# A chunked delta rule with and without the product w: k'S taken off the values in place, under new order tables

## The reference, cut to what matters

```python
decay = exp(where(tri, g[:, None] - g[None, :], -inf))       # g: running sum of the log decay
lower = where(strict, beta[:, None] * (k @ k.T) * decay, 0)
rhs   = concat([v * beta, k * (beta * exp(g))])
u, w  = split(triangular_solve(lower, rhs, unit_diagonal=True))
# from chunk to chunk, S is the 128 x 256 state of the head:
v_new = u - w @ S
o     = (q * exp(g)) @ S + (q @ k.T * decay) @ v_new
S     = S * exp(g_last) + (k * exp(g_last - g)).T @ v_new
```

## Time and profile before

| | |
|---|---|
| median of three runs | 1504.52 us |
| profiled execution | 1505.05 us, its span 1503.2 us |
| granted TensorE clock, mean | 0.996 |
| TensorE busy | 1482.1 us, 99% of the span |
| VectorE, ScalarE, POOL busy | 62%, 49%, 17% |
| DMA | 127.21 MB, mean 85 GB/s |

### The profile page before, as it was taken

How to read it: one execution, slowest core, us unless ns; L and a number is a source line. 1 busy time by engine, 2 the same in 40 slices (tenths; PEclk the granted TensorE clock), 3 DMA queues, 4 the chain that set the end, 5 groups by cost and what they waited for, 6 DMA issues and landing times.

```text
span 1503.2 us, 20571 instructions
## 1 busy us (share of the span) xinstructions
PE 1482.1 (99%) x7595; PEld 1186.4 (79%) x7595; DVE 924.7 (62%) x1740; ACT 736.4 (49%) x1292; POOL 261.9 (17%) x430
## 2 busy tenths in 40 slices
PE   9999999999999999999998999999999999999998
PEld 7878888888778878888877887666778888888887
DVE  5867777777655468788886346554475243433467
ACT  5454455544552356666665234665455341423343
POOL 1034323344302015354430000000000000000000
PEclk9999999999999999999999999999999999999999
DMA  5321211121114342222321332121233233232321
GB/s 210 99 71 60 68 57 56 57 62 51 57 57 146 112 111 95 76 93 79 92 78 57 99 100 63 59 68 42 87 95 99 85 112 98 85 101 96 98 84 70
DMA packets 40163, 127.21 MB, mean 85 GB/s; under 512 B 4576, under 2 KB 9104, under 8 KB 40064
## 3 DMA queue, kind: packets, MB, share of 16 engines
q1 hardware_dynamic: 38112, 121.65, 25.6%
q0 software_dynamic: 1040, 3.27, 0.6%
q10 hardware_dynamic: 912, 0.99, 0.2%
HBM read 122.69 MB, written 2.15 MB: 83 GB/s over the span
## 4 chain that ended last, share of the span: by engine, by line
PE 91%; DVE 4%; ACT 3%; issue 1%; DMA 0%; POOL 0%; SPq 0%; DVEq 0%; ACTq 0%; POOLq 0%
PE ps L891 89%; PE ps L1292 1%; DVE wl L2058 1%; PE ps L1036 1%; ACT sp L1954 1%; ACT sp L1952 0%; ACT sp L1956 0%; ACT wh L1439 0%; DVE up L2212 0%; DMA wraw<-in_wa 0%; DVE xr L2648 0%; ACT xr L1719 0%; DVE L L2600 0%; PE ps L1131 0%; ACT L1680 0%
## 5 line engine op out<-in xcount | busy, mean ns | idle before, releaser
L891 PE MATMUL ps<-xr,wh 128*128 128x512 f32 x2720 | 875.1, 402 | 3.4 <-DVE xr L2648 2.4
L891 PEld LDWEIGHTS ps<-xr,wh 128*128 128x128 f32 x2720 | 498.1, 189 | 119.9 <-issue 22.2
L891 PE MATMUL ps<-xr,wl 128*128 128x512 f32 x1376 | 538.6, 391 | 0.0
L2058 DVE TENSOR_TENSOR wl<-wraw,wh 128x1024 fp32r<-128x1024 f32 x214 | 268.2, 1260 | 131.6 <-ACT wh L1439 130.6
L891 PEld LDWEIGHTS ps<-xr,wl 128*128 128x128 f32 x1376 | 258.7, 188 | 55.6
L1439 ACT ACTIVATE wh<-wraw 128x1024 fp32r<-128x1024 f32 x214 | 222.1, 1049 | 74.4 <-PE ps L891 73.0
L891 PE MATMUL ps<-xm,wh 128*128 128x512 f32 x640 | 197.8, 390 | 0.0
L891 PEld LDWEIGHTS ps<-xm,wh 128*128 128x128 f32 x640 | 119.5, 188 | 26.2 <-DVE xm L2734 1.6
L891 PE MATMUL ps<-xm,wl 128*128 128x512 f32 x320 | 124.6, 389 | 0.0
L2096 DVE SCALAR_TENSOR_TENSOR qkv<-cin,gains,qkv 128x512 f32<-128x512 f32 x96 | 76.0, 792 | 10.0 <-ACT qkv L1469 9.3
L2919 POOL TENSOR_TENSOR L<-L 128x256 f32<-128x256 f32 x44 | 49.5, 1149 | 147.2 <-ACT L L1855 147.2
(11 more groups left out here) (292 smaller groups left out, 1763.9 us busy)
## 6 DMA issues: line engine op xcount, KB each, us to landing
wraw<-in_wa SPq DMA_DIRECT2D x48, 512.0 KB, 3.5
wraw<-in_wb SPq DMA_DIRECT2D x32, 512.0 KB, 4.2
wraw<-in_wu SPq DMA_DIRECT2D x32, 512.0 KB, 3.5
wraw<-in_wd SPq DMA_DIRECT2D x32, 512.0 KB, 3.6
wraw<-in_wao SPq DMA_DIRECT2D x16, 512.0 KB, 3.6
wraw<-in_wbo SPq DMA_DIRECT2D x16, 512.0 KB, 4.2
wraw<-in_wc SPq DMA_DIRECT2D x16, 512.0 KB, 3.5
bias<-rel_rows SPq DMA_DIRECT2D x16, 256.0 KB, 3.8
```

Source lines behind the costliest of these rows:

```text
L891: return e.matmul(out, w, x, start=start, stop=stop, skip_group_check=True)
L2058: e.tensor_tensor(m.wl[:, i % N_SPLIT, :], m.raw[:, i % N_RAW, :], m.wh[:, i % N_SPLIT, :].bitcast(F), ALU.subtract).then_inc(s.wlo, 1)
```

## The change

The product w, its scaling kg and its copy wT go. Normalised k is kept in a tile of its own (`kc`, two buffers; before it was written back over the head's k). At chunk n >= 1 a new product *k* multiplies it with the state (256 columns, the upper half of bank 4), and VectorE adds it, times the negative decay `egn`, to the values in place (*v*, one `scalar_tensor_tensor` of 128 x 256). Then r is U'v alone. The recurrence has 14 items instead of 11, `levels` 8 instead of 9, and four tables are new.

```diff
-    "a2": plan("p0 p5 p2 q0 p2 q4 q1 q2 q0 p0 q2 q0 p1 q1 q0 p3 r0 p1 r0 r1 p0 r0 r1 p1 r0 r3 r0 r0 p4 r0 p0 p4 p0 r6"),
-    "a8": plan("p0 q2 p0 q3 q1 q1 p0 q0 p2 q0 p0 q0 p1 q1 q0 p1 r1 r0 r1 p0 r0 r0 p2 p0 r0 p0 p0 r3 r4 r0 p0 p0 r1 r2"),
-    "a9": plan("q1 q5 q2 q5 q2 q1 q3 q2 q5 r7 r0 r1 r0 r2 r0 r2 r1 r3 r2 r4"),
-    "a": plan("p0 q2 q0 p4 q1 q0 p1 p0 q3 q2 p0 q1 p0 q1 q1 p0 r2 r2 r0 p2 r0 p2 r1 p0 p2 r2 r1 r2 r1 p1 r2 p2 p2 r14"),
+    "a2": plan("p0 p4 p2 q0 p1 q2 q1 q1 q0 p0 q2 q1 p0 q1 p0 r1 p0 r1 r1 r1 p1 r1 r1 r1 p0 r1 r2 r1 r2 p2 p2 r0 r3 p2 p1 r5"),
+    "a8": plan("p0 q2 p0 q2 q1 q1 p0 q0 p2 q0 p0 q1 p0 q1 p0 r0 p0 r1 r1 r1 p0 r0 r1 r1 p0 r1 p0 r1 p0 r1 r2 p1 r0 p0 r2 r2"),
+    "a9": plan("q1 q5 q2 q5 q2 q1 q3 q1 r2 r1 r2 r1 r1 r2 r1 r1 r2 r2 r3 r3 r3 r4"),
+    "a": plan("p0 q2 q0 p4 q1 q0 p1 p0 q3 q2 p0 q1 p0 q1 p0 r1 p1 r1 r2 r1 p1 r1 r2 r1 p1 r1 r2 r2 r2 p2 p1 r0 r2 p1 p1 r4"),
...
-STEPS = {"gates": 4, "prep": 14, "levels": 9, "recur": 11, ...
+STEPS = {"gates": 4, "prep": 14, "levels": 8, "recur": 14, ...
...
 # TensorE, levels
-        e.wait_ge(s.lev_a, lev_a(h, "TF"))
-        end(four(bank(), lambda n: m.kg[:, n, :], lambda n: m.U[:, par, n, :]), (s.lev_a, lev_a(h, "w")))
-        yield
...
 # TensorE, recur, for n in range(4)
             if n == 0:
-                e.wait_ge(s.lev_a, lev_a(h, "w"))
-            ins = mm(m.banks[4][:, 0:256], m.U[:, par, n, :], m.vt[:, par, n, :], True, n == 0)
-            if n:
-                e.wait_ge(s.rec_v, REC_V * h + n)
-                ins = mm(m.banks[4][:, 0:256], m.wT[:, par, n, :], so, False, True)
-            ins.then_inc(s.rec_p, 1)
+                e.wait_ge(s.lev_v, lev_v(h, "U6"))
+                e.wait_ge(s.prep_a, prep_a(h, "v1"))
+            else:
+                if n == 2:
+                    e.wait_ge(s.lev_a, lev_a(h, "TF"))
+                e.wait_ge(s.rec_v, rec_v(h, f"S{n}"))
+                mm(m.banks[4][:, 256:512], m.kc[:, par, ts], so).then_inc(s.rec_p, 1)
+                yield
+                e.wait_ge(s.rec_v, rec_v(h, f"v{n}"))
+            mm(m.banks[4][:, 0:256], m.U[:, par, n, :], m.vt[:, par, n, :]).then_inc(s.rec_p, 1)
...
 # ScalarE, levels: the copy goes
-        did(e.activation(m.wT[:, par], m.bk(LEV_BANK), ACT.Copy))
...
 # ScalarE, recur, for n in range(4)
+            if n:
+                yield
+            e.wait_ge(s.rec_p, rec_p(h, f"r{n}"))
...
 # VectorE, prep
-        did(e.tensor_tensor(k, k, m.rq[:, 0, :], ALU.mult))
+        free_of_recurrence()
+        did(e.tensor_tensor(m.kc[:, par, :], k, m.rq[:, 0, :], ALU.mult))
...
-        did(e.tensor_tensor(m.kg[:], o, bc(m.egn[:, col]), ALU.mult))
         did(e.tensor_tensor(m.kd[:, par], o, bc(m.ekd[:, col]), ALU.mult))
...
 # VectorE, recur, for n in range(4)
+            if n:
+                v = m.vt[:, h % 2, n, :]
+                e.wait_ge(s.rec_p, rec_p(h, f"k{n}"))
+                did(e.scalar_tensor_tensor(out=v, in0=m.banks[4][:, 256:512], scalar=m.egn[:, 4 * h + n:4 * h + n + 1],
+                                           in1=v, op0=ALU.mult, op1=ALU.add))
+                yield
```

More of the change, by code:

```diff
@@ L590, in __init__ @@
         self.qd = a.new([2, 512], name="qd")
-        self.kg = a.new([4, 128], name="kg")
         self.kd = a.new([2, 4, 128], name="kd")
         self.vt = a.new([2, 4, 256], name="vt")
-        self.wT = a.new([2, 4, 128], name="wT")
+        self.kc = a.new([2, 512], name="kc")
         self.W = a.new([2, 8, 128], name="W")
@@ L806 @@
     ("silu1", "sqk", "silu0", "silu2", "silu3", "lnk", "exk", "eb", "E", "sqq", "v0", "v1"))}
-PREP_V = {n: i + 1 for i, n in enumerate(("dv", "y", "at", "qk", "kg", "kd", "dc", "X", "qdn", "U3", "T3"))}
+PREP_V = {n: i + 1 for i, n in enumerate(("dv", "y", "at", "qk", "kd", "dc", "X", "qdn", "U3", "T3"))}
 PREP_O = {n: i + 1 for i, n in enumerate(("sel", "D"))}
 N_INV = 31
-LEV_P = {n: i + 1 for i, n in enumerate(("P4", "U4", "P5", "U5", "T5", "P6", "U6", "TF", "w"))}
-LEV_A = {n: i + 1 for i, n in enumerate(("P4", "P5", "T5", "P6", "TF", "w"))}
+LEV_P = {n: i + 1 for i, n in enumerate(("P4", "U4", "P5", "U5", "T5", "P6", "U6", "TF"))}
+LEV_A = {n: i + 1 for i, n in enumerate(("P4", "P5", "T5", "P6", "TF"))}
 LEV_V = {n: i + 1 for i, n in enumerate(("U4", "T4", "U5", "U6"))}
 LEV_O = {n: i + 1 for i, n in enumerate(("M4", "M5", "M6"))}
-REC_P, REC_A, REC_V = 12, 8, 9
+REC_P = {n: i + 1 for i, n in enumerate(
+    ("r0", "d0", "o0", "k1", "r1", "d1", "o1", "k2", "r2", "d2", "o2", "k3", "r3", "o3", "sum"))}
+REC_V = {n: i + 1 for i, n in enumerate(("S1", "v1", "S2", "v2", "S3", "v3", "q0", "q1", "g0", "g1", "f0", "f1"))}
+REC_A = 8
 STICK_P = {n: i + 1 for i, n in enumerate(
@@ L851, in lev_o, with rec_p, rec_v @@
     return len(LEV_O) * h + LEV_O[name]
+def rec_p(h, name):
+    return len(REC_P) * h + REC_P[name]
+def rec_v(h, name):
+    return len(REC_V) * h + REC_V[name]
 def stick_p(j, name):
@@ L1041, in prep @@
         par = h % 2
-        q, k = m.qkv[:, par, 0, :], m.qkv[:, par, 1, :]
+        q, k = m.qkv[:, par, 0, :], m.kc[:, par, :]
         ch = [slice(n * 128, (n + 1) * 128) for n in range(4)]
@@ L1175, in recur @@
         for j in range(2):
[L1176 removed]
+            clear[6 + j] = [(s.rec_a, REC_A * h + 5 + j), (s.rec_v, rec_v(h, f"g{j}"))]
         yield
         cleared(5)
[L1179 removed]
+        e.wait_ge(s.rec_v, rec_v(h, "q1"))
         mm(m.banks[5][:], m.ones, m.sqh[:, 0, :]).then_inc(s.rec_p, 1)
@@ L1699, in recur @@
         for j in range(2):
-            e.wait_ge(s.rec_p, REC_P * h + 11)
+            e.wait_ge(s.rec_p, rec_p(h, "o3"))
             if h:
-                e.wait_ge(s.rec_v, REC_V * h)
+                e.wait_ge(s.rec_v, rec_v(h - 1, "f1"))
             did(e.activation(m.sqh[:, j, :], m.banks[6 + j][:], ACT.Square))
         yield
-        e.wait_ge(s.rec_p, REC_P * h + 12)
+        e.wait_ge(s.rec_p, rec_p(h, "sum"))
         if h == 0:
@@ L1729, in square @@
             e.wait_ge(s.olo, 16)
-            e.wait_ge(s.rec_p, REC_P * HEADS)
+            e.wait_ge(s.rec_p, len(REC_P) * HEADS)
             e.wait_ge(s.prep_o, len(PREP_O) * HEADS)
@@ L2363, in free_of_recurrence @@
             if h >= 2:
-                e.wait_ge(s.rec_p, REC_P * (h - 2) + 11)
+                e.wait_ge(s.rec_p, rec_p(h - 2, "o3"))
         yield from idle(3)
@@ L2458, in recur @@
             if n < 3:
-                e.wait_ge(s.rec_p, REC_P * h + 3 * n + 2)
+                e.wait_ge(s.rec_p, rec_p(h, f"d{n}"))
                 if n:
-                    e.wait_ge(s.rec_p, REC_P * h + 3 * (n - 1) + 3)
-                    e.wait_ge(s.rec_v, REC_V * h + n)
+                    e.wait_ge(s.rec_p, rec_p(h, f"o{n - 1}"))
+                    e.wait_ge(s.rec_v, rec_v(h, f"S{n}"))
                     did(e.scalar_tensor_tensor(out=sn, in0=so, scalar=m.egl[:, 4 * h + n:4 * h + n + 1],
@@ L2855, in levels @@
         masked(m.Mm[:, 0], m.X[:], m.masks[:, 6, :]).then_inc(s.lev_o, 1)
-        yield from idle(8)
+        yield from idle(7)
     def invert(h):
```

29 lines of the change are left out of this document (10 added, 19 removed).

## The result

The changed kernel takes 1555.14 us (median of 4 runs, 1553.70 to 1556.53), the kernel before 1504.75 in the same session: a ratio of 1.0333, 95% interval 1.0321 to 1.0345. The profiled run took 1553.7 us, with a span of 1551.9; that is 12.7 us above the 1541 that the forecast gives against the profiled run, and 3 above the top of the range. The sign and the place of the loss are those of the forecast, and so are the waits; the size is not.

A forecast was written before the change was run, and what follows sets the result against it. TensorE, busy 1482.1 of 1503.2 us, was taken as the bound; new waits less savings gave 25.5 (middle heads) + 6.6 (first) + 3.4 (seventh) + 0.7 (last) = +36 us, 1540.5 as a median, range 1520 to 1550.

The forecast's parts named there:

- Term (1), the k transposes: Middle heads: k transposes wait 0.9 us for the bank that VectorE empties into qkT.
- Term (2), k1 behind S: Middle heads: d0 to k1 has only d0 and o0 as cover, then a drain without matmuls; 0.3 us wait.
- Term (3), r3 behind v3: Middle heads: v3 is queued on VectorE behind the third drain's tap and wl, so r3 waits 0.3 us.
- Term (4), "The norm sum": Middle heads: squares queue behind qkv and wh, VectorE's additions follow, so TensorE waits 4.7 us at the sum.
- d0 of the last head: Last head: ScalarE's gate with two table loads precedes the first rtmp, so d0 waits 2.25 us.
- v0 of the seventh: Seventh head: v transposes wait 1.75 us for kd, held up by an opening's wh and wl.
- the clock falls: Rival: long norm-sum waits bring half-pace matmuls, 15.5 us for five, half of that giving 1548; chance 0.15.
- a mean granted clock still near 0.99: Sign expected in the after trace, over the whole kernel, if the forecast held.
- No wait at the norm sum: Rival: cin, wh and squares run early enough that q1 is ready; +10 us, 1514.5; chance 0.13.
- faster: Rival: every link is covered by its step and other heads' work, TensorE only relieved; 1496.5; chance 0.08.
- cancelled: Rival: waits of about 1 us a head leave the time at 1504.5; chance 0.04.
- The saving: All eight heads: removing w saves 0.98 us of TensorE a head, 7.8 us; with small ScalarE-copy waits, 8.6.

The follow-up runs named there:

- e2: Changed kernel with five extra 512-column fp32 matmuls, unneeded work, put on TensorE before the norm sum of the five middle heads; 1544.50 us.
- e1: Changed kernel with only the middle heads' table edited: squares two items earlier, ahead of two preparation items; 1536.51 us, ratio to before 1.0213.
- e8: Changed kernel with two extra 512-column matmuls before each of the five middle heads' norm sums, filling the wait in part; 1549.75 us, ratio 1.0290.
- e4: Changed kernel with all four tables laid out anew, in the middle heads with most steps between o3 and the squares moved behind the squares; 1530.67 us, ratio 1.0173.
- e7: Changed kernel, tables re-laid repeatedly, adds and gate as own items; last edit: middle heads' chain from second state update one step earlier; 1508.61 us, ratio 1.0022.
- e3: Kernel before, product w kept, with only the middle heads' table edited so the last output comes as late as in the changed kernel; 1538.41 us, ratio 1.0226.
- e9: Changed kernel with one swap in the middle heads' table: first recurrence product r0 ahead of the k transposes; 1556.05 us, ratio 1.0335.
- e5: Changed kernel with tables laid out again, VectorE's two adds and gate as own items, norm sum ahead of the head's last evacuation; 1520.26 us, ratio 1.0109.

## Why the prediction was right, and where it was wrong

**The sign and the four waits of a middle head: right.** The list counts a wait from the modelled end of the matmul ahead of it (0.39 us long), but TensorE could have started the next one after 0.23. The forecast counts from start to start, and so must the answer. The rows above give it for the sum; these give it for the other three:

```profile
173.99 0.40 PE L901 MATMUL ps<-xr,wl 128*128 128x512 f32 x1
175.14 0.66 PE L1046 MATMUL ps<-k,kc 128*128 128x128 f32 x4 [0.76 <-DVE qkT L2389]
...
178.34 0.61 PE L901 MATMUL ps<-qkT,rtmp 128*128 128x128 f32 x4
179.11 0.67 PE L901 MATMUL ps<-S,kc 128*128 128x256 f32 x2 [0.17 <-DVE S L2478]
...
192.07 0.40 PE L901 MATMUL ps<-xr,wl 128*128 128x512 f32 x1
192.55 0.70 PE L901 MATMUL ps<-vt,W 128*128 128x256 f32 x2
```

- Term (1), the k transposes: 175.14 - 173.99 - 0.23 = 0.92 (0.9 forecast).
- Term (2), k1 behind S: 179.11 - 178.34 - 4 x 0.11 = 0.33 (0.3).
- Term (3), r3 behind v3: 192.55 - 192.07 - 0.23 = 0.25 (0.3).
- Term (4), "The norm sum": 202.82 - 197.88 - 0.23 = 4.71 (4.7); the chain that makes it was right to 0.05 us.

Together 6.2, as forecast. By the same count d0 of the last head waits 2.3 (2.25 forecast) and v0 of the seventh 1.9 (1.75).

**The sums of the parts.** Against the profiled run the forecast is 12.7 us short:
- First head: +6.6 forecast, +7.9 measured. Its norm sum was put at 1.4 and waits for 2.4; the rest is not assigned.
- Five middle heads: 25.5 forecast. Of the measured 37.4, 9.9 are the low clock; 27.5 are left, 5.5 a head. The forecast left out that each product behind a wait also starts more slowly (0.06 to 0.10 us, last section), 0.3 a head for four of them, and it took off 0.1 a head for small waits of before, of which no trace shows a gain. 6.2 + 0.3 - 0.98 = 5.5.
- Seventh and last head: 3.4 + 0.7 = 4.1 forecast, 3.8 measured.

So 1.3 + 2.0 - 0.3 - 0.3 (the start) are errors in size, and 9.9 is the step that failed.

**The step that failed.** It is the rival "the clock falls", which got 0.15 and no term in the sum. The forecast held against it that "the page shows no such stretch later". That was a misreading: a digit of the page's row PEclk is the mean of 38 us, and 9 stands for 90% or more. The trace of before has such stretches, behind a wait of 1.34 us that ends at 785.82 and one of 2.43 that ends at 801.89:

```profile
786.00:789.00 3.00, 1.79 (x6) 1.09 (x6) 1.25 (x3) 1.99 (x4) 0.00 (x0) 0.50 0.56 175
803.00:806.00 3.00, 3.00 (x9) 2.13 (x7) 2.86 (x7) 2.85 (x4) 1.64 (x3) 0.51 0.49 173
```

So waits half as long as the forecast five were already followed by the low clock, and the rival had the better evidence. e2 shows that it is the standstill that brings it, and it came at all five sums of the changed kernel. Its price was bounded well: 15.5 us at the most and half of that as the guess, against 9.9 to 10.6 measured, near 2 us a wait. The Trainium skill (TensorE: Matmul & The Clock Gate, Part 1), cited in the prediction, says that an idle TensorE falls to 1.2 GHz and needs sustained work to come back. The windows agree with both: 0.58 at the end of a wait without a matmul, and 0.50, then 0.95 in the next 4 us of work, at the first dip. e1 and e8 show that a wait of 2.3 to 2.7 us brings it only sometimes. The range ended at 1552 because it took the clock's dearest case out; with the dips in the sum the forecast would have been 1540.5 + 10 = 1550.5. Of the signs that it named, a mean granted clock still near 0.99 could not tell: it came out at 0.989 with the dips in it. The other could: it named a pitch of 0.46 us behind a wait, and behind the second sum a matmul follows the one before after 0.43 us (258.04 to 258.46) instead of 0.23.

**"No wait at the norm sum", "faster", "cancelled".** All wrong for this table. e4 to e7 show what they would have needed: not only another place for the squares, but another order on VectorE, since at each edit the wait turned up at another consumer: the sum, then rq, then S, then v and rtmp.

**The saving.** 0.98 us a head for w, 7.8 in all, stays an estimate: no run took w away alone. In e7 a middle head is 0.2 us longer than before. Its two listed waits (0.35 and 0.26) are 0.51 and 0.40 from start to start, and four products start more slowly, some 0.33 in all: 45.45 before, less 45.68 - 0.91 - 0.33 = 44.44, leaves about 1.0, in line with the estimate.

## What to carry to other kernels

When a chain gets longer by a link, lay out the queue of every engine up to the last consumer before trusting that cover exists: here VectorE, idle for 40% of the span, and ScalarE, idle for 53%, were full in the few microseconds that mattered, and each repaired wait moved to the next consumer. A wait on the engine that sets the time has two prices, its length and what the clock does behind it. A mean over the span or over 38 us can't speak against the second (0.996 before, with the clock at 0.50 from 786 to 789 us); windows of 3 us around the waits of before can, and they put it in the sum here. Putting the old kernel on the new table (e3) tells in one run whether the arithmetic or its placing costs.

## What the runs showed of the hardware

- **The low clock comes with a standstill, in its last part or behind it, and not every time.** Behind waits of 4.55 us the granted clock was 0.50 to 0.66 in all fifteen cases (changed kernel, e3, e9). Behind 2.74 us it was low three times in five (e8), behind 2.3 us three times in five (e1), behind 2.51 us five times in five (e4, 0.55 to 0.66). Behind the five waits of 1.58 us in e5 it stayed at 1.00; yet in the kernel before it was 0.50 from 786 us on, right behind a wait of 1.34 us, where TensorE was busy for 0.66 of the 2 us from 784. The first head's wait of 2.3 us, the same in five kernels, left the clock at 1.00 in the changed one and in e1 and was followed by 0.60 in e2, 0.64 in e8 and 0.50 in e9. What decides it the runs don't show.
- **More work can be faster.** 25 products that nobody needs (e2) took 10.6 us off the time.
- **A start behind a wait costs a little more than the wait.** The pair of 512-column products on rq takes 0.86 us to the next start before (240.94 to 241.79), 0.93 in e7 behind a wait of 0.26 (243.15 to 244.08); the 256-column pair behind 0.35 us takes 0.53 (221.41 to 221.94), otherwise 0.43.
- **The list of waits is 0.16 us short at each wait of TensorE.** A matmul of 512 columns shows a length of 0.39 us where the next one starts 0.23 after it (197.65 to 197.88), so the listed 4.56 at the sum is 4.71 from start to start.
